# The last matrix product of a decoder layer, from plain tiles to quads of seven block products

## The reference, cut to what matters

```
x = x + 0.5 * swiglu(rms_norm(x, ffn1_norm), ffn1_w_gu, ffn1_w_down)      # D_FF = 2816
x = x + concat([window_attention(q, k, v), pool(u)]) @ w_out              # token mixer
x = x + 0.5 * swiglu(rms_norm(x, ffn2_norm), ffn2_w_gu, ffn2_w_down)
gate = sigmoid(rms_norm(x, ple_norm) @ ple_w_gate + ple_b_gate)           # 1024 x 1024
e = rms_norm(p @ ple_w_proj, ple_post_norm)
x = x + gate * e                                                          # 1024 tokens x 1024
```

## Time and profile before

| what | value |
|---|---|
| median of 3 runs | 1667.97 us |
| profiled execution, its own time | 1667.36 us |
| span of the profiled execution | 1665.6 us |
| PE busy | 1654.2 us (99%) |
| DVE busy | 1211.7 us (73%) |
| ACT busy | 683.4 us (41%) |
| POOL busy | 301.7 us (18%) |
| granted TensorE clock | 0.999 of full (2.4 GHz) |

### The profile page before, as it was taken

How to read it: one execution, slowest core, us unless ns; L and a number is a source line. 1 busy time by engine, 2 the same in 40 slices (tenths; PEclk the granted TensorE clock), 3 DMA queues, 4 the chain that set the end, 5 groups by cost and what they waited for, 6 DMA issues and landing times.

```text
span 1665.6 us, 20613 instructions
## 1 busy us (share of the span) xinstructions
PE 1654.2 (99%) x7384; PEld 1345.4 (81%) x7384; DVE 1211.7 (73%) x1805; ACT 683.4 (41%) x1120; POOL 301.7 (18%) x343
## 2 busy tenths in 40 slices
PE   9999999999999999999999999999999999999998
PEld 6788888888888888886777888888888888888887
DVE  7998887888655768578776798778677653666763
ACT  7534333343344444356644343333323324434431
POOL 0023333233100000144320003333334100000000
PEclk9999999999999999999999999999999999999999
DMA  9068777777579764353446316676545349876465
GB/s 333 29 228 316 277 270 271 272 259 264 206 261 365 220 200 154 127 177 103 133 141 226 108 38 250 249 259 238 197 187 187 140 151 328 284 247 190 160 213 176
DMA packets 135357, 351.12 MB, mean 211 GB/s; under 512 B 12549, under 2 KB 54029, under 8 KB 126936
## 3 DMA queue, kind: packets, MB, share of 16 engines
q1 hardware_dynamic: 119288, 297.59, 51.7%
q0 software_dynamic: 12832, 46.46, 8.0%
q10 hardware_dynamic: 3136, 5.77, 0.9%
HBM read 245.42 MB, written 105.92 MB: 211 GB/s over the span
## 4 chain that ended last, share of the span: by engine, by line
PE 92%; DVE 5%; ACT 2%; DMA 1%; issue 1%; SPq 0%; ACTq 0%; DVEq 0%
PE bank L920 30%; PE bank L921 29%; PE bank L922 29%; DVE qb L1996 1%; PE bank L1183 1%; PE bank L1195 1%; PE bank L1135 1%; DMA x_sb<-in_xT 1%; DVE hn L1604 0%; DVE acc L1592 0%; PE bank L951 0%; DVE dn_lo L1825 0%; DVE probs L2020 0%; ACT dn_hi L1334 0%; DVE x_sb L1624 0%
## 5 line engine op out<-in xcount | busy, mean ns | idle before, releaser
L1825 DVE TENSOR_TENSOR dn_lo<-d_f,dn_hi 128x1024 fp32r<-128x1024 f32 x154 | 185.0, 1221 | 125.0 <-ACT dn_hi L1334 124.6
L920 PE MATMUL bank<-h_hi,t_hi 128*128 128x512 f32 x704 | 274.8, 390 | 0.0
L922 PE MATMUL bank<-h_hi,t_lo 128*128 128x512 f32 x704 | 273.9, 389 | 0.0
L921 PE MATMUL bank<-h_lo,t_hi 128*128 128x512 f32 x704 | 273.9, 389 | 0.0
L920 PE MATMUL bank<-dn_hi 128*128 128x512 f32 x616 | 241.1, 391 | 0.7 <-DVE dn_lo L1825 0.7
L922 PE MATMUL bank<-dn_hi,dn_lo 128*128 128x512 f32 x616 | 239.7, 389 | 0.0
L921 PE MATMUL bank<-dn_lo,dn_hi 128*128 128x512 f32 x616 | 239.7, 389 | 0.0
L1334 ACT ACTIVATE dn_hi<-d_f 128x1024 fp32r<-128x1024 f32 x154 | 159.9, 1056 | 162.6 <-DMA d_f<-in_wd 89.3
L891 POOL TENSOR_TENSOR wdr<-wdr 128x256 f32<-128x256 f32 x176 | 172.5, 980 | 224.8 <-DMA wdr<-in_wd 214.4
L920 PE MATMUL bank<-c_hi,t_hi 128*128 128x512 f32 x544 | 211.6, 389 | 0.0
L921 PE MATMUL bank<-c_lo,t_hi 128*128 128x512 f32 x544 | 211.6, 389 | 0.0
(11 more groups left out here) (174 smaller groups left out, 2426.3 us busy)
## 6 DMA issues: line engine op xcount, KB each, us to landing
raw<-in_gu SPq DMA_DIRECT2D x44, 1024.0 KB, 5.3
d_f<-actc SPq DMA_DIRECT2D x154, 256.0 KB, 3.4
actc<-acts SPq DMA_DIRECT2D x20, 1792.0 KB, 6.8
w_hi<-hl SPq DMA_DIRECT2D x52, 512.0 KB, 4.3
w_lo<-hl SPq DMA_DIRECT2D x52, 512.0 KB, 5.2
wdr<-in_wd POOLq DMA_DIRECT2D x44, 512.0 KB, 5.1
wdc<-wdr POOLq DMA_DIRECT2D x44, 512.0 KB, 3.4
d_f<-wdc SPq DMA_DIRECT2D x88, 256.0 KB, 3.3
```

What stands on the lines that cost most here:

```text
L920: pe.matmul(ps, whi, vhi, start=first, stop=False, skip_group_check=onto)
L921: pe.matmul(ps, whi, vlo, start=False, stop=False, skip_group_check=onto)
L922: return pe.matmul(ps, wlo, vhi, start=False, stop=last, skip_group_check=onto)
L1825: dve.tensor_tensor(dn_lo[slot][:, :], d_f[slot][:, :], plain(dn_hi[slot][:, :]), ALU.subtract).then_inc(dn_split, 1)
```

## The change

The gate becomes four quads (output tile pairs j = 0 to 3) of seven block products: 28 products of 12 matmuls. Its operands are sums of normed token tiles (made on VectorE, those of Q5 and Q3 on GpSimd) and of weight blocks. The sums of weight blocks are made on VectorE beside ffn2's quads (`sum_unit`), so there are 14 units instead of 8: four "p" of plain blocks (quads 4 to 7), four "a" with three sums from two loads of 512 KB (quads 8 to 11), four "b" with two sums from three loads of 256 KB (quads 12 to 15), two "c" of plain blocks (quads 16 and 17). GpSimd scales `e` (16 multiplications) and adds 12 of the 16 outputs to x. `e` is loaded in 16 pieces into a ring of six. Products are gathered in all eight banks.

```
+GATE_SEQ = [(P1, 0), (P1, 1), (P1, 2), (P2, 0), (P1, 3), (P2, 1), (P2, 2), (P2, 3)]
+GATE_SEQ += [(s, j) for s in (Q4, Q6, Q7, Q5, Q3) for j in range(GQ)]
+GATE_UNITS = [("p", j) for j in range(GQ)] + [("a", j) for j in range(GQ)] + [("b", j) for j in range(GQ)]
+GATE_UNITS += [("c", 0), ("c", 1)]
+POOL_OUTS = 3 * GQ
...
             def split_load(u):
                 if u:
                     sp.wait_ge(unit_out, 32 * u)
...
+                elif kind == "a":
+                    sp.dma_start(unit_f[:, :], first).then_inc(unit_in, 16)
+                    sp.dma_start(unit_g[:, :], second).then_inc(unit_in, 16)
+                elif kind == "b":
+                    sp.dma_start(unit_f[:, one], second[:, one]).then_inc(unit_in, 16)
+                    sp.dma_start(unit_f[:, two], first[:, one]).then_inc(unit_in, 16)
+                    sp.dma_start(unit_g[:, one], second[:, two]).then_inc(unit_in, 16)
...
# VectorE, in quad(): between w3 and the next low parts
                     make_w3(ph, q)
+                if 0 <= q - U_QUAD[ph] < len(SPLITS[ph]):
+                    sum_unit(SPLITS[ph][q - U_QUAD[ph]])
                 for x in todo[1:3]:
                     split_t(ph, *x)
                 if q > 2:
                     make_c22(ph, q)
...
+            def sum_unit(u):
+                if not UNIT_SUMS[u]:
+                    return
+                dve.wait_ge(unit_in, unit_loaded(u))
...
+                for i, (to, term) in enumerate(steps_of[GATE_UNITS[u - U_GATE0][0]]):
+                    if i:
+                        dve.wait_ge(unit_summed, sum(UNIT_SUMS[:u]) + i)
+                    dve.tensor_tensor(to, to, term, ALU.add).then_inc(unit_summed, 1)
...
# SyncE, after ffn2
+            for n in range(SLOTS):
                 store(n)
+                e_load(n + E_RING)
+                gate_load(2 * SLOTS + n)
+            for n in range(SLOTS, 2 * GQ):
+                store(n)
+                e_load(n + E_RING)
+                if n % 2:
+                    gate_load(3 * SLOTS + (n - SLOTS) // 2)
...
# GpSimd, after scale_e(0..3) and the eight sums for Q5 and Q3
+            for n in range(POOL_OUTS):
...
+                pool.wait_ge(gate_gated, n + 1)
+                pool.tensor_tensor(x, x, eg[n % E_RING][:, :], ALU.add).then_inc(y_pool, 1)
+                if n + GQ < 4 * GQ:
+                    scale_e(n + GQ)
```

More of the change, by code:

```diff
@@ L257 @@
 BANK7 = [("norm", 0), ("norm", 1)]
[L258 removed]
+BANK7 += [s for s in PLAN if s[0] in ("norm", "qks", "vt")] + [("norm", 5)]
 BANK7_AT = {s: i for i, s in enumerate(BANK7)}
@@ L541, in h_count, with gate_count, gate_copied, gs_count @@
         def h_count(nrm, k):
-            return KT * H_AT[nrm] + k + 1
+            return KT * H_AT[nrm] + (TOK1_POS[k] if nrm == 7 else k) + 1
+        def gate_count(s, j):
+            return len(MAIN) + GATE_AT[(s, j)] + 1
+        def gate_copied(j):
+            return sum(kind == "act" for kind, _ in FREED) + j + 1
+        def gs_count(s, kk):
+            return h_count(7, TOK1_ORDER[KH - 1]) + GATE_S_AT[(s, kk)] + 1
+        def mixed_count(what, j):
+            return MIX_AT[(what, j)] + 1
+        def unit_loaded(u):
+            return 16 * sum(UNIT_LOADS[:u + 1])
+        def wait_out(engine, n):
+            if n < POOL_OUTS:
+                engine.wait_ge(y_pool, n + 1)
+            else:
+                engine.wait_ge(y_made, n - POOL_OUTS + 1)
         def sq_count(nrm, i):
@@ L1232, in _, with gate_operand @@
             ffn(1)
[L1234 to L1241, removed]
+            def gate_operand(s, kk):
+                if s in (P1, P2):
+                    k = kk + KH * (s == P2)
+                    return h_hi[0][:, k, :], h_lo[0][:, k, :]
+                if s == Q4:
+                    return h_hi[1][:, KH + kk, :], h_lo[1][:, KH + kk, :]
+                return gs_hi[s][:, kk, :], gs_lo[s][:, kk, :]
@@ new lines, in _ @@
+            for n, (s, j) in enumerate(GATE_SEQ):
+                m, half = gate_part(s, j)
+                pe.wait_ge(*unit_ready(U_GATE + m))
+                wait_gate_bank(s, j)
+                for kk in range(KH):
+                    if j == 0:
+                        if s in (P1, P2):
+                            pe.wait_ge(h_split, h_count(6, kk + KH * (s == P2)))
+                        elif s == Q4:
+                            pe.wait_ge(h_split, h_count(7, KH + kk))
+                        else:
+                            pe.wait_ge(h_split, gs_count(s, kk))
+                    c = slice((half * KH + kk) * P, (half * KH + kk + 1) * P)
+                    hi, lo = gate_operand(s, kk)
+                    last = three(gate_bank(s, j)[:, :], w_hi[m % SLOTS][:, c], w_lo[m % SLOTS][:, c], hi, lo,
+                                 kk == 0 and s not in (P2, Q3), kk == KH - 1, s in (P2, Q3))
+                last.then_inc(main_made, 1)
+                if n == GATE_SUM:
+                    norm_sum(7)
@@ L1576, in _ @@
+            for j in range(GQ - 1):
+                gate_copy(j)
+            std(7)
+            gate_sigmoid(0)
+            gate_copy(GQ - 1)
+            for k in TOK1_ORDER[:KH]:
+                round_h(7, k)
+            gate_sigmoid(1)
+            gate_round(Q6)
+            gate_sigmoid(2)
+            gate_round(Q7)
+            gate_sigmoid(3)
+            gate_round(Q5)
+            gate_round(Q3)
+            for n in range(GQ, 4 * GQ):
+                gate_sigmoid(n)
         @block.vector
@@ new lines, in _ @@
+            gate_split(Q6, [KH - 1])
+            gated_out(1)
+            gate_split(Q7, range(KH))
+            gated_out(2)
+            gate_w2(0)
+            gate_split(Q5, (0, 1))
+            gated_out(3)
+            gate_w2(1)
+            gate_split(Q5, (2, 3))
+            gate_w2(2)
+            gate_split(Q3, (0, 1))
+            gate_w2(3)
+            gate_split(Q3, (2, 3))
+            for j in range(GQ):
+                gate_w3(j)
+                if j:
+                    gated_out(GQ + j - 1)
+                gate_c21(j)
@@ L2068, in build @@
+            for j in range(GQ):
+                gate_c22(j)
+                gated_out(2 * GQ + j - 1)
+            for j in range(GQ):
+                gate_c12(j)
+                gated_out(3 * GQ + j - 1)
+            gated_out(4 * GQ - 1)
 def build(nc, xT, pT, units, gu, wd, poolw, small, const, onehot, rel, out):
```

312 lines of the change are left out of this document (230 added, 82 removed).

## The result

The changed kernel takes 1708.87 us (median of 6 runs, 1691.63 to 1714.06) against 1667.49 us (6 runs, 1667.31 to 1668.77): a ratio of 1.0234, 95% interval 1.0207 to 1.026. The forecast was 1672.3 us with a range up to 1682. The direction was right, the size was not.

The account below looks back on a forecast made before the run. TensorE, busy 99% of the span, was taken to bound the kernel. Terms -10.9 + 1.2 + 11.5 + 2.5 = +4.3 us gave 1671.7, and 1672.3 us with the runs' median 0.6 higher; range 1661 to 1682.

Parts of the forecast that it names:

- -10.9 for 48 matmuls: Gate on TensorE: 336 matmuls instead of 384, at 0.2267 us each, save 10.9 us.
- Quads +11.5: Quads 8 to 15: TensorE waits for c22 behind late weight loads, 9.3 us, plus 2.2 us for GpSimd collisions.
- the limit of 12.3 us: Quad 8: both unit loads must land within 12.3 us of the quad's start, or c22 makes Q3 late.
- Landings: Unit loads in quads 8 to 15: 1.4 us for each further 512 KB; late landings make up the 9.3 us.
- The lock: Operations ahead of c22 in the stalled quads: GpSimd's additions slow VectorE's, 2.2 us in all (0 to 7).
- The clock: Rival 4, chance 0.08: TensorE at 1.2 GHz after waits in four even quads, 11 us, 1683 us.
- Gate's loads +2.5: Gate at Q7: the four "b" units' weights arrive late for TensorE, 2.5 us (0 to 5).
- At nothing: Gate: half 1's norm and GpSimd's work, eight sums included, stay covered by one to three us, costing nothing.
- Tail +1.2: Kernel's end on VectorE: from the last product to the last addition 3.4 us instead of 2.2, 1.2 us more.
- Rival 1: Quads: loads land by the limit and the sums are hidden, quads cost 0 to 3.4 us; 1660.5 us, chance 0.20.
- Rival 2: Quads: each even quad pays only its own lateness, 5.6 us, and the next begins afresh; 1665 us, chance 0.20.
- Rival 3: Gate: GpSimd at 1.62 us an operation delays the first output and the first "b" load, +4 us, 1676 us, chance 0.07.

Follow-up runs that it names:

- e9: e7 with Q3's four sums behind the third w2, its low parts beside w3, and the "c" loads ahead of stores 5 and 6: 1662.69 us.
- e12: e1 with c22 worked out twelve more times in quads 4, 6, 18 and 20, so TensorE waits there: 1698.04 us.
- e3: The changed kernel without the loads into `unit_g` for "a" and "b" units; the sums add halves of `unit_f`: 1694.64 us.
- e11: e1 with c22 worked out seven more times in quads 4, 6, 18 and 20, so TensorE waits there: 1677.5 us.
- e1: The changed kernel with the sums of weight blocks moved behind four more low parts, just ahead of c21: 1669.13 us.
- e6: e1 with the eight sums for Q5 and Q3 on VectorE instead of GpSimd: 1665.17 us.
- e5: e1 with the gate's four "b" weight loads issued ahead of the stores instead of behind them: 1668.38 us.
- e7: e1 with the edits of e5 and e6 together: 1665.05 us.
- e8: The changed kernel with the unit's loads issued ahead of the 1792 KB store of activations in ffn2's even quads: 1684.49 us.

## Why the prediction was wrong, point by point

- **-10.9 for 48 matmuls: right.** It is in e9's gate, which takes 78.35 us from first to last matmul against 87.72; with its wait of 0.85 us and some 0.7 elsewhere the 9.4 us are 10.9.
- **Quads +11.5: the step that failed.** It cost 32.4 us of waits and 12.5 more, 44.9 us. The path was right: the limit of 12.3 us, the loop over the last unit's stores (in by +7.9 in quad 9, where I had +7.3), the even quads worst. The odd ones were not free: 1.23 us in quad 9 and 2.92 in quad 15. Three parts of the term were wrong, two in size and one in kind:
  - *Landings.* In quad 8 `unit_g` landed 9.5 us after its issue, at 1111.1, not 1109.5, with the quad itself 0.5 later: 1.1 us more. In quad 10 (from 1142.12) it was issued at +7.8 and took 10.6: +18.4, where I had +15.8. The store of activations there landed at +13.4, and the two loads 2.6 and 2.4 us behind it and each other, where I had 1.4 for each. The "b" quads missed by more. Quads 12 and 14 had their last piece at +18.7 and +19.0, where I had +15.1 and +14.0. In quad 15 (from 1268.48), which I had on time, the last unit's stores were in at +9.6 and not at +7.3, and the last piece came at +16.0, 3 us late. With 1.0 us in quad 9, landings are about 16 of the 23 us by which the waits went beyond my 9.3.
  - *The lock,* as I call VectorE and GpSimd holding each other up. Landing to end of c22 took 5.6, 5.8, 5.2 and 5.2 us in the four even quads, where I had 4.0, 4.0, 3.3 and 3.3. I put it down as 2.2 us in all; it was 7.2. Quad 8: 2.1 + 1.1 + 1.6 is its 4.8. Quad 10: 6.1 past the limit and 1.8 are about its 7.83.
  - *The clock.* I made it a rival, with a chance of 0.08 and 11 us of its own. It isn't a rival: it follows the forecast's own kind of wait, as e12 shows, and so belonged in the sum as soon as a wait of 3.5 us stood in it. By my own numbers only quad 10 was that long; by the measured ones five were 2.9 us or more, and the wider spacing behind them is 10.5 us. That this is near the rival's 11 us is luck: it was worked out for one product behind each of four quads.
  
  The page "TensorE: Matmul & The Clock Gate" of the Trainium skill (Part 1) says that an idle engine is throttled until it has been busy again; the rows at 1116.00 and e12 agree, while the clock stayed at 1.00 behind 3.58 us in e3 and 3.32 in e11. "SBUF — State Buffer" of the Trainium skill ("Who interferes with whom") has GpSimd and VectorE exclude each other when the VectorE operation has both inputs in SBUF; e1 against e6 agrees (1.77 us against 0.69). Both rules pointed to the higher times.
- **Gate's loads +2.5: about right in the wait,** 3.2 us for `w_lo`; the 1.7 us of wider spacing behind it were not in the sum. Its reason isn't settled: with the loads ahead of the stores (e5) 3.4 us stayed, which speaks for what the queue can move, as I argued; in e9 0.85 stayed, with other work around it.
- **"At nothing", GpSimd's eight sums: wrong.** They cost three waits, 2.6 us, for `gq_lo`, and 1.7 us of half-clock matmuls behind; e6 took both away, though a wait of 2.04 us came ahead of Q7. I had timed them at 1.38 us each and left out what they do to VectorE.
- **Tail +1.2: too small.** From c12's start it was 3.46 us (3.4 forecast), but c12 itself came 1.1 us late, behind VectorE operations of 1.67 and 1.18 us (0.69 and 0.74 where GpSimd was done): +2.3. In e9 it is +4.4.
- **Sum.** -10.9 + 2.3 + 44.9 + 10.3 (the gate's waits and its two stretches at half clock, worked out as the rest: 87.16 - 87.72 + 10.9) is +46.7, which is 1714.06 - 1667.36.

Rival 1, hidden sums, fails in this kernel; in e1, where the limit of 12.3 us is gone, the quads are as it had them, though the whole is 1669.13 us and not 1660.5. Rival 2 fails: the delays fed on. Rival 3, GpSimd pacing the gate, is half seen: in e1 its eight sums took 1.7 to 2.0 us each, and the first "b" load went out at 1613.5, about 3.5 us after my 1610. But e5 took that load out from behind the store and won 0.3 us, so the path by `store(0)` is not what held it.

Open: which waits bring the clock down (2.04 us did in e11 and 1.98 in e7, while 2.15 in e11, 2.04 in e6, 3.32 in e11 and 3.58 in e3 did not); why the stores in quad 15 took 2.3 us longer than I had; and how much of the spread of the changed kernel's runs (1691 to 1714) is landings and how much the clock.

## What to carry to other kernels

On an engine that runs in order, place a wait for a load behind everything that the bottleneck engine needs soon: the same additions cost 44.9 us ahead of c22 and nothing behind it. When a forecast has TensorE wait several us, put the matmuls at 1.2 GHz behind the wait into the sum as well: here they cost 1.5 to 2.9 us behind 25 of the 27 waits of 2.9 us and more. Take landing times from a trace with the new traffic in it, or widen the range for them: a further load landed 2.0 to 2.4 us behind the last where 1.4 had been taken. Work moved to GpSimd is not free for VectorE: compare the pair's durations side by side, since here VectorE alone was faster than both.

## What the runs showed of the hardware that was not expected

- From 1000 us on, the profiles of the changed kernel and of the twelve experiments hold 27 waits of TensorE of 2.9 us and more. Behind 25 of them some 7 to 14 matmuls start about 0.43 us apart instead of 0.2267, 1.5 to 2.9 us more. Behind two they do not (3.58 us in e3, 3.32 in e11). Of the nine waits from 1.4 to 2.2 us two were followed by it (2.04 in e11, 1.98 in e7). The three for `gq_lo`, 0.59, 1.31 and 0.73 us, close together, were followed by it in e1 and not in e12.
- Two streams of additions on SBUF, one on each engine, take 1.77 us on VectorE (0.69 alone) and 1.7 to 1.99 on GpSimd (1.29 alone), about the sum of the two times alone.
- A unit's last load (512 or 256 KB) behind a store of 1792 KB and its other loads landed 9.3 to 10.6 us after its issue in the even quads of the changed kernel; in its odd quads, which have no such store, 4.4 to 5.6, and in e8, with the store behind it, 3.8 to 6.4.
